# Products of ones by ones in three layer norms and in front of the router of a two-block model

## The reference, cut to what matters

```python
def layer_norm(x, g, b):
    mu = jnp.mean(xf, axis=-1, keepdims=True)
    var = jnp.mean(jnp.square(xf - mu), axis=-1, keepdims=True)
    y = (xf - mu) * lax.rsqrt(var + LN_EPS)
    ...
for i in range(DEPTH):                                  # first block
    ...
    x = layer_norm(DN_ALPHA * x + (1.0 + gate) * y, ln_g[i, 0], ln_b[i, 0])
    y = sq_relu_mlp(x * (1.0 + scale) + shift, mlp_w1[i], mlp_w2[i])
    x = layer_norm(DN_ALPHA * x + (1.0 + gate) * y, ln_g[i, 1], ln_b[i, 1])
...
hx2 = modulate(rmsnorm(x, norm2_g[layer]), mod_x[3], mod_x[4])     # second block
probs = jax.nn.softmax(h @ router_w, axis=-1)           # 16 experts in 4 groups
best_group = jnp.argmax(group_score, axis=-1)           # one group, two experts in it
out = out + combine[:, e:e + 1] * (jax.nn.silu(h @ w_gate[e]) * (h @ w_up[e])) @ w_down[e]
```

## Time and profile before

| | |
|---|---|
| median of 3 runs | 1405.18 us (1405.04 to 1406.17) |
| the profiled execution | 1403.54 us, of which the span is 1402.0 us |
| TensorE matmul busy | 1301.4 us (93%) |
| VectorE busy | 1023.3 us (73%) |
| ScalarE busy | 704.8 us (50%) |
| mean granted TensorE clock | 0.959 |

### The profile page before, as it was taken

One profiled execution on the slowest core, in us unless ns is written; L12 is line 12 of the kernel. 1 busy time (PEld: TensorE's weight loads), 2 busy tenths in 40 slices (PEclk: granted clock), 3 DMA queues, 4 the chain that ended last, 5 costly groups with the idle time before them and its releaser, 6 DMA issues.

```text
span 1402.0 us, 19912 instructions
## 1 busy us (share of the span) xinstructions
PE 1301.4 (93%) x7796; PEld 1165.9 (83%) x7796; DVE 1023.3 (73%) x1462; ACT 704.8 (50%) x968; POOL 0.4 (0%) x5
## 2 busy tenths in 40 slices
PE   6988799999998897899999899998899999999996
PEld 6777799999887787899998688998788877878775
DVE  5676686877658976787777758775767779688685
ACT  3432444453367773444453543432557657566563
POOL 0000000000000000000000000000000000000000
PEclk9968999999999999999999999999899999999998
DMA  8728787777285765777652542310448879788772
GB/s 333 263 73 322 269 316 281 273 276 273 98 307 211 273 207 191 282 262 279 232 190 75 189 150 76 105 61 12 150 159 305 306 232 331 260 296 295 236 256 87
DMA packets 82685, 308.17 MB, mean 220 GB/s; under 512 B 9312, under 2 KB 9568, under 8 KB 81824
## 3 DMA queue, kind: packets, MB, share of 16 engines
q1 hardware_dynamic: 80352, 292.59, 58.2%
q10 hardware_dynamic: 2240, 14.31, 2.6%
HBM read 305.82 MB, written 1.05 MB: 219 GB/s over the span
## 4 chain that ended last, share of the span: by engine, by line
PE 75%; DVE 16%; DMA 4%; ACT 3%; issue 2%; SPq 0%; ACTq 0%; DVEq 0%
PE ps L465 74%; DVE w_low L424 4%; DMA ring<-stream 3%; DVE junk L424 3%; ACT w_high L424 1%; DVE t_one L424 1%; DVE rs L424 1%; DVE ti L424 1%; DVE x L424 1%; PE ps L1120 1%; DVE hsc L424 1%; DVE y_experts L424 1%; DMA ring<-moe 0%; DVE x_low L424 0%; DVE r_two L424 0%
## 5 line engine op out<-in xcount | busy, mean ns | idle before, releaser
L424 DVE TENSOR_TENSOR w_low<-ring,w_high 128x1024 fp32r<-128x1024 f32 x368 | 441.9, 1221 | 148.4 <-ACT w_high L424 146.1
L424 ACT ACTIVATE w_high<-ring 128x1024 fp32r<-128x1024 f32 x368 | 386.2, 1058 | 309.9 <-PE ps L465 179.3
L465 PE MATMUL ps<-x_high,w_high 128*128 128x256 f32 (+1 forms) x816 | 242.4, 297 | 32.2 <-DVE x_low L424 23.1
L465 PE MATMUL ps<-x_high,w_low 128*128 128x256 f32 (+1 forms) x816 | 239.0, 293 | 0.0
L465 PE MATMUL ps<-x_low,w_high 128*128 128x256 f32 (+1 forms) x816 | 239.0, 293 | 0.0
L424 DVE CUSTOM_DVE_ANT_0 junk<-ring,cond 128x1024 f32<-128x1024 f32 x137 | 166.9, 1222 | 37.1 <-DMA ring<-stream 28.6
L465 PEld LDWEIGHTS ps<-x_high,w_high 128*128 128x128 f32 x816 | 159.2, 195 | 40.6 <-issue 22.7
L465 PEld LDWEIGHTS ps<-x_low,w_high 128*128 128x128 f32 x816 | 159.0, 195 | 1.7
L465 PEld LDWEIGHTS ps<-x_high,w_low 128*128 128x128 f32 x816 | 158.3, 194 | 1.7
L465 PE MATMUL ps<-h_high,w_high 128*128 128x256 f32 x512 | 144.3, 282 | 3.1 <-DVE h_low L424 2.7
L465 PE MATMUL ps<-h_high,w_low 128*128 128x256 f32 x512 | 144.7, 283 | 0.0
(11 more groups left out here) (318 smaller groups left out, 1945.2 us busy)
## 6 DMA issues: line engine op xcount, KB each, us to landing
ring<-stream SPq DMA_DIRECT2D x364, 512.0 KB, 5.2
ring<-moe SPq DMA_DIRECT2D x192, 512.0 KB, 5.0
gw<-gw ACTq DMA_DIRECT2D x1, 3840.0 KB, 14.6
tab_two<-tab ACTq DMA_DIRECT2D x1, 2824.0 KB, 14.9
cond<-cvec ACTq DMA_DIRECT2D x2, 512.0 KB, 5.4
x<-xT ACTq DMA_DIRECT2D x1, 1024.0 KB, 11.7
ctx_first<-ctxT ACTq DMA_DIRECT2D x1, 1024.0 KB, 4.8
ctx<-ctxT ACTq DMA_DIRECT2D x1, 1024.0 KB, 4.7
```

Of the source, the lines that this page charges most:

```text
L424: return op(*a, **k).then_inc(self.sem, by)
L465: return pe.matmul(out, stationary, moving, start=start, stop=stop, skip_group_check=True)
```

## The change

A new helper `keep_on(n)` in TensorE's program issues n products of the ones matrix with itself, 128 by 128 with 128 columns, into PSUM bank 3, whose result nobody reads. They wait for nothing and signal nothing. Six stand between the mean and the sum of squares in the norms 0, 1 and 2; eighteen stand behind the sum of squares in the norms 0 and 2, in front of `mlp`; thirteen stand behind the router's sum of squares, in front of the logits. Together these are 67 products.

```diff
+    def keep_on(n):
+
+        for _ in range(n):
+            mm(PS[:, 3, 0:P], m.ONES, m.ONES, True, True)
+
     def layer_norm(r, between=()):
 
         for k in range(KT):
             pe.wait_ge(s.x_add, 8 * r + max(k, 1) + 1)
             ins = mm(m.MEAN, m.ONES, m.X[:, k, :], k == 0, k == KT - 1)
         ins.then_inc(s.mean_mm, 1)
+        if r < 3:
+            keep_on(6)
         context_steps(between)
...
     layer_norm(0)
+    keep_on(18)
     mlp(W_MLP0, 0, 8, x_splits(MOD_LN0) + 1)
...
     layer_norm(2)
+    keep_on(18)
     mlp(W_MLP1, 8, 8, x_splits(MOD_LN2) + 1)
...
     square_sums(SQ_MOE, PS[:, 7, 0:256], m.T2, KT)
+    keep_on(13)
```

## The result

The changed kernel took 1394.1 us (median of 8 executions, 1392.5 to 1397.4) against 1404.8 us for the kernel before in the same measurement; the ratio is 0.994, with a 95% interval of 0.992 to 0.996. A second measurement of the unchanged pair gave 1393.7 us and 0.995 (0.993 to 0.997). The prediction was 1402.0 us, with 1399.8 to 1404.9 as its range: the sign was right, the size was less than half of what came.

The account below looks back on a forecast made before the run. TensorE's stream of products was taken to bound the kernel, with waits and slow clock behind them left at the change. Gains of 0 + 0.8 + 0.2 + 2.2 = 3.2 us from 1405.2 gave 1402.0 us, range 1399.8 to 1404.9.

Parts of the forecast that it names:

- the base: Whole kernel: the starting time from which the gains were subtracted, a median of 1405.18 us.
- the silent term: Rest of the kernel, away from the added products: no gain or loss was included for it.
- the three places: Norm 0, norm 2 and the router, where the forecast put gains of 0.8, 0.2 and 2.2 us.
- The second rival: All groups: ones by ones don't hold the clock, so it falls where it fell, 1405.2 us; chance 0.06.
- The third: All groups: clock already low, groups outlast their waits, 5.4 us slower, 1410.6; slower forms together 0.04.
- The first: Norm 0 and router: clock falls anyway, early in the logits; only 1.1 us gained, 1404.1; chance 0.20.
- Sixes: Between mean and sum of squares, norms 0, 1, 2: clock hadn't fallen there, so 0 us.
- Norm 0: Eighteen before its MLP: TensorE gains 0.8 to 2.4 us, later landings absorb part; 0.8 us, ends 0 and 2.4.
- Norm 2: Eighteen before its MLP: 2.8 us stays idle, clock should fall again; 0.2 us, ends -0.5 and 1.4.
- Router: Thirteen before the logits: most logits at full clock, identity products perhaps slower; 2.2 us, ends -1.7 and 3.4.
- The sum: Whole kernel: 0 + 0.8 + 0.2 + 2.2 = 3.2 us gained.
- The range: Whole kernel: 1399.8 us with 2.0 + 3.4 us gained, to 1404.9 with the small gain and median scatter.

Follow-up runs that it names:

- eighteens_only: Only the two groups of eighteen products, behind norms 0 and 2, added to the kernel before; its times couldn't be told from no change.
- after_again: The changed kernel, unchanged, measured a second time beside the kernel before: 1393.7 us, ratio 0.995.
- norms_full_again: Second run of the kernel before plus full-width sixes and eighteens, nothing at the router; its two runs together were 1.3 us under the mean of before.
- before_third: The kernel before, unchanged, run and traced a third time; 1395.6 us, where the first trace of the same code has 1402.0.

## Why the prediction was right or wrong, point by point

Two steps failed: the base, a median of three executions, which was 3.7 us above the kernel's mean, and the silent term for all that lies outside the three places, put at nothing and measured at 3.5 us. Together with the 0.7 us by which the places gave more than their sum, these are the 7.9 us between 1402.0 and 1394.1. Why the second term isn't nothing stays open.

**Sign, and the rivals.** The sign was right. The second rival, that ones by ones hold nothing, is out: behind the full-width form the clock was 1.00 at norm 0 in all seven traces that have it and 0.94 in the logits of the changed kernel; at norm 2, where the eighteen leave 2.64 us idle, it held in two traces of five. The third, that a group lasts longer than its wait, is out: 1.46, 2.64 and 0.51 us are left in front of the three, where 1.6, 2.8 and 0.6 were worked out. The first, a smaller gain, is out in the times.

**The base.** The sum was made against 1405.18 us, and the text noted that the profiled execution was 1.6 us faster and that slow stretches vary by such amounts, but it took the median of three as the kernel's time. Its mean is 1401.5 us. With it, the forecast would have been 1398.3 us. Starting from three executions that all lay in the slow part of the scatter was bad luck; to take them for the kernel's time was the step that failed.

**Sixes: 0.** Right; 1400.6 us, 0.9 under the mean of before with an error of 0.8, and the sums of squares still take 3.72 us.

**Norm 0: 0.8, ends 0 and 2.4.** TensorE gained 2.3 us, near its upper end, since the clock held over the 1.46 us left. Nothing of it arrived, which is the term's lower end. The failed step is the amount that the landing of pieces would let through: the prediction named the right limit, but read it at the `w_high` of 184.60 and the `w_low` of 186.13, where 1.5 us of VectorE's delay could go first. The piece that bound is the one before, the `w_high` of 179.96, which ScalarE took up 30.41 us behind `t_one` before and could not take up sooner after (31.28 us). In the row of before it shows no wait, and so it looked free.

**Norm 2: 0.2, ends -0.5 and 1.4.** It gave 1.0 us between the traces of the two kernels and 0.5 us over all traces, within its ends. The reason was off: the clock was expected to fall again behind 2.8 us of idle time. It held in the changed kernel's profile behind 2.64 us, and fell behind the same wait in the profiles of `eighteens_only`, `after_again` and `norms_full_again`. The length of the wait, from which the prediction drew, doesn't decide by itself: at 1.80, 2.16 and 2.64 us both outcomes occur.

**Router: 2.2, ends -1.7 and 3.4.** It gave 2.85 us, but not by the terms of the working. The logits took 4.42 us, within the 3.4 to 5.5 that were named, the clock fell behind most of them, and the products with the identity went slow, which gave back 1.2 us (1.7 was the bound). These two, the only ones that the working had, come to 1.4 us. The other 1.5 us were left out: they come from the slow stretch near 1022 us, which wasn't there.

**The sum: 3.2 us.** The places gave 0 + 0 + 1.0 + 2.85 = 3.9 us. The number is close, in part by luck: norm 0 gave 0.8 us less than its term, norm 2 gave 0.8 us more though its reason was off, and half of the router's gain stands at a stretch that no term had.

**Elsewhere: 0, unsaid.** This is the other step that failed. Everything outside the three places was taken to stay as it was. It was 3.5 us faster in the means of executions. In one trace this can be chance, as `before_third` shows; over 17 executions of the changed kernel it stays (3.5 us), while its two parts, with 24 each, show 1.4 us (router) and 0.3 to 0.8 us (norms) beyond their places, and with the one-column form it is there though the places gain next to nothing. Half-clock time elsewhere is the same to within 0.8 us in the traces, so that isn't the answer. Why is open.

**The range.** Its low end, 1399.8 us, had 5.4 us of gain in it, less than came, but the base alone would have moved it to 1396.1. It was also narrower than its own terms: their upper ends, 0 + 2.4 + 1.4 + 3.4, come to 7.2 us, and it counts 2.0 of the norms' 3.8 without saying why. The range was built from the terms alone; a base taken from three executions of a kernel that scatters by 10 us needs a term of its own.

## What to carry to other kernels

Where TensorE waits in a dense stream (the waits here were 1.8 to 6.7 us long), products that nobody reads, 128 columns wide, can keep its clock for what comes behind, and cost nothing while they end inside the wait; the less of the wait they leave idle, the surer (2.64 us left: held in two traces of five; nothing left: in two of two). The gain counts only where no transfer binds next, so look also at the rows that show no wait, and ask when their data came. Take the time of a kernel from dozens of executions, and several traces, before a difference under 1% is split into causes: one trace of the same code can differ from the next by more than the effect. After three places are filled, try the others: here a longer group and three more gave another 4.9 us (six executions).

## What the runs showed of the hardware that was not expected

- A matmul record of one column takes about as long as one of 128 columns (0.126 against 0.118 us in the waits at the router), keeps TensorE busy, and doesn't keep the clock: 0.50 to 0.53 behind it, 1.00 or 0.94 behind the full-width form.
- The same wait in the same code, 1.80, 2.16 or 2.64 us long, is followed by 1.00 in one execution and by a stretch at 0.50 to 0.57 in another. The kernel before scatters from 1396.0 to 1406.9 us over all series, and the time of an execution goes with its half-clock time (correlation 0.86 over 173 executions).
- Behind thin products the clock fell without any wait. The logits, 16 columns wide, ran at 0.94 behind the full-width products, and the products with the identity behind them at 0.53. Behind the 20 products 4 columns wide, which stand in the middle of dense work, it fell in twelve of the twenty traces and held in eight. That their width is the cause is likely, but no run changes it.
